# The byte positions of a weight ring in SBUF, moved stage by stage

## The reference

```python
# first block
z = rmsnorm(x) @ w_in                          # 1024 -> 4608
a = silu(layernorm(conv31(a_val * sigmoid(a_gt)))); y_a = a @ w_a_out
s = sc_b * conv3(sc_c * sc_v);                      y_b = s @ w_b_out
x = x + (sigmoid(.) * y_a + sigmoid(.) * y_b) @ w_o
u = rmsnorm(x) @ w_up                          # 1024 -> 2 * 2816
x = x + (gelu(conv3(u[:2816])) * u[2816:]) @ w_down
x = x + sigmoid(rmsnorm(x) @ w_ple_gate) * (p @ w_ple)
x = rmsnorm(x)
# second block
proj = rmsnorm(x) @ w_in_2                     # 1024 -> 2304, two kinds of attention
x = x + rmsnorm(attention(proj) @ w_out_2)
u = conv3(rmsnorm(x) @ w_up_2)                 # 1024 -> 2 * 4096
x = x + rmsnorm((gelu(u[:4096]) * u[4096:]) @ w_down_2)
```

## The kernel before

| operand | before | after |
|---|---|---|
| weights of in, b_out, ple, a_out, o | 96 | 80 |
| weights of up, down | 96 | 48 |
| weights of gate, in2, out2 | 96 | 72 |
| weights of up2 and the first three units of down2 | 96 | 56 |
| weights of the other 29 units of down2 | 0 | 0 |
| chunks h, h2 (also the operand of o) and f | 0 | 0 |
| chunks s, a, p and y | 64 | 0 |

## Time and profile before

### The profile page before, as it was taken

The page is one execution under the profiler, slowest core; times in us unless marked ns, Lnnn a source line. Parts: engine busy times, 40 slices in busy tenths (PEclk is TensorE's granted clock), DMA queues, the critical chain, the costliest instruction groups (busy, mean ns, idle before and its releaser), DMA issues. The chain is left out here.

```text
span 790.7 us, 17002 instructions
## 1 busy us (share of the span) xinstructions
PE 763.4 (97%) x5986; PEld 735.0 (93%) x5986; DVE 584.8 (74%) x1051; ACT 449.0 (57%) x752; POOL 259.6 (33%) x159
## 2 busy tenths in 40 slices
PE   8999999999999999999899998799999999999996
PEld 8999999999999999999788887699999999988885
DVE  6899967668888885436866785679999999963333
ACT  7554555566565664446744565576666666653441
POOL 0376642462122213345480011822211222122220
PEclk9999999999999999999999999899999999999999
DMA  8566554556555576644343332535555555666551
GB/s 278 160 213 197 189 161 146 190 184 191 192 181 194 184 236 210 193 138 143 131 133 109 106 108 77 165 107 186 189 187 185 189 187 187 218 201 196 188 171 53
DMA packets 37772, 135.46 MB, mean 171 GB/s; under 512 B 4448, under 2 KB 4704, under 8 KB 37728
## 3 DMA queue, kind: packets, MB, share of 16 engines
q1 hardware_dynamic: 37728, 134.86, 52.3%
HBM read 133.80 MB, written 1.05 MB: 171 GB/s over the span
## 5 line engine op out<-in xcount | busy, mean ns | idle before, releaser
L1655 PE MATMUL bank<-h_hi,w_hi 128*128 128x256 f32 x1424 | 403.7, 283 | 9.2 <-DVE h_lo L1072 6.5
L1656 PE MATMUL bank<-h_lo,w_hi 128*128 128x256 f32 x1424 | 399.1, 280 | 0.0
L1657 PE MATMUL bank<-h_hi,w_lo 128*128 128x256 f32 x1424 | 398.9, 280 | 0.0
L718 ACT ACTIVATE w_hi<-raw 128x1024 fp32r<-128x1024 f32 (+2 forms) x246 | 262.1, 1067 | 92.4 <-PE bank L1657 43.1
L553 POOL TENSOR_TENSOR w_lo<-raw,w_hi 128x1024 fp32r<-128x1024 f32 (+1 forms) x75 | 186.4, 2487 | 383.9 <-ACT w_hi L718 383.6
L1060 DVE TENSOR_TENSOR w_lo<-raw,w_hi 128x1024 fp32r<-128x1024 f32 (+2 forms) x171 | 218.3, 1279 | 104.4 <-ACT w_hi L718 104.3
L1655 PEld LDWEIGHTS bank<-h_hi,w_hi 128*128 128x128 f32 x1424 | 269.5, 189 | 16.2 <-issue 9.1
L1656 PEld LDWEIGHTS bank<-h_lo,w_hi 128*128 128x128 f32 x1424 | 269.7, 189 | 0.0
L1657 PEld LDWEIGHTS bank<-h_hi,w_lo 128*128 128x128 f32 x1424 | 269.4, 189 | 0.0
L1100 DVE TENSOR_TENSOR bank<-bank,scales 128x256 f32<-128x256 f32 x124 | 53.0, 431 | 27.8 <-PE bank L1657 13.9
L1328 DVE TENSOR_TENSOR f_lo<-src,f_hi 128x256 f32 (+1 forms) x54 | 60.7, 1124 | 0.5 <-ACT f_hi L866 0.5
(11 more groups left out here) (203 smaller groups left out, 914.4 us busy)
## 6 DMA issues: line engine op xcount, KB each, us to landing
raw<-in_w_up SPq DMA_DIRECT2D x108, 512.0 KB, 3.3
raw<-in_w_in SPq DMA_DIRECT2D x54, 512.0 KB, 3.4
raw<-in_w_down SPq DMA_DIRECT2D x32, 512.0 KB, 4.2
raw<-in_w_down SPq DMA_DIRECT2D x16, 704.0 KB, 4.1
raw<-in_w_o SPq DMA_DIRECT2D x8, 512.0 KB, 3.3
raw<-in_w_gate SPq DMA_DIRECT2D x8, 512.0 KB, 3.5
raw<-in_w_out SPq DMA_DIRECT2D x8, 512.0 KB, 3.3
raw<-in_w_b_out SPq DMA_DIRECT2D x4, 512.0 KB, 3.6
```

The source lines that it names most:

```text
L718: nc.scalar.activation(w_hi[s][:, cols], raw[s][:, cols], ACT.Copy).then_inc(hi_ready, 1)
L1655: nc.tensor.matmul(ps, wh, hi[:, k, :], start=start and n == 0, stop=False)
L1656: nc.tensor.matmul(ps, wh, lo[:, k, :], start=False, stop=False)
L1657: last = nc.tensor.matmul(ps, wl, hi[:, k, :], start=False, stop=stop and n == len(ks) - 1)
```

## The change

The ring gets another position, and that position another one for each stage. `w_hi` and `w_lo` become slices of one tensor `w_all` whose first slot starts 48 bytes past a multiple of 128 (`RING_COL = 12` floats); `first_col` adds 8, 0, 6, 2 or 20 floats by the stage, and now counts in every load, rounding, subtraction and product. `raw` lies behind `w_all` and uses the same columns. Large tensors start at multiples of 128 instead of 64 bytes, which moves s, a, p and y (table above). Four pairs of small scratch values share two tensors (`lam`, `o_small`). No instruction is added or removed, and the order, the semaphores and all shapes stay. The rest of the diff passes the unit instead of its slot to `products`, in every call.

```diff
@@ -55,12 +55,18 @@
 
 WARM_UP = 16
 
-RING_PAST = 32
+RING_COL = 12
 
 
 def first_col(u):
 
-    return RING_PAST // 4 if u >= UNIT0["down2"] + LEAD else 0
+    if u < UNIT0["up"]:
+        return 8
+    if u < UNIT0["gate"]:
+        return 0
+    if u < UNIT0["up2"]:
+        return 6
+    return 2 if u < UNIT0["down2"] + LEAD else 20
 
 
 def unit_blocks(u):
@@ -267,15 +273,15 @@
         at = [(nc.sbuf_base + 31) // 32 * 32]
 
         def aligned(offset, size):
-            step = 64 if size >= 1024 else 32
+            step = 128 if size >= 1024 else 32
             return (offset + step - 1) // step * step
 
-        def sb(name, shape, dt=f32, offset=None, past=0):
+        def sb(name, shape, dt=f32, offset=None, small=False):
 
             size = 4 * math.prod(shape[1:])
             if offset is not None:
                 return nc.alloc_sbuf_tensor_at(name, shape, dt, offset=offset)
-            at[0] = aligned(at[0] - past, size) + past
+            at[0] = aligned(at[0], 0 if small else size)
             t = nc.alloc_sbuf_tensor_at(name, shape, dt, offset=at[0])
             at[0] += size
             return t
@@ -285,8 +291,8 @@
         gg = sb("gg", [P, DC])
...
         UNIT_MAX = max(b for _, _, b in PHASES) * P
-        raw = [sb(f"raw{i}", [P, UNIT_MAX], past=RING_PAST) for i in range(RING)]
-        w_hi = [sb(f"w_hi{i}", [P, UNIT_MAX], f32r, past=RING_PAST) for i in range(RING)]
-        w_lo = [sb(f"w_lo{i}", [P, UNIT_MAX], f32r, past=RING_PAST) for i in range(RING)]
+        ring_at = (at[0] - 4 * RING_COL + 127) // 128 * 128 + 4 * RING_COL
+        w_at = ring_at - ring_at % 32
+        w_all = sb("w_all", [P, 2 * RING * UNIT_MAX + 8], f32r, offset=w_at)
+        w_first = [(ring_at - w_at) // 4 + UNIT_MAX * i for i in range(2 * RING)]
+        w_hi = [w_all[:, w_first[i]:w_first[i] + UNIT_MAX] for i in range(RING)]
+        w_lo = [w_all[:, w_first[RING + i]:w_first[RING + i] + UNIT_MAX] for i in range(RING)]
+        at[0] = w_at + 4 * (2 * RING * UNIT_MAX + 8)
+        raw = [sb(f"raw{i}", [P, UNIT_MAX], small=True) for i in range(RING)]
         X = sb("X", [P, DC, TOK])
         branch = sb("branch", [P, DC, TOK])
         h_hi = sb("h_hi", [P, DC, TOK], f32r)
-            load("in", 0, (0, None))
+            load("in", 0, (0, None), first_col(0))
...
-                    load(name, i, (slot(base + i), (base + i) // RING))
+                    load(name, i, (slot(base + i), (base + i) // RING), first_col(base + i))
...
-            def products(ps, s, block0, ks, hi, lo, start, stop, ready=None):
+            def products(ps, u, block0, ks, hi, lo, start, stop, ready=None):
 
                 for n, k in enumerate(ks):
                     if ready is not None:
                         pe.wait_ge(*ready(k))
-                    b = block0 + n
-                    wh, wl = (w[s][:, b * P:(b + 1) * P] for w in (w_hi, w_lo))
+                    col = first_col(u) + (block0 + n) * P
+                    wh, wl = (w[slot(u)][:, col:col + P] for w in (w_hi, w_lo))
...
-                    products(bank[slot(t)][:, 0:TOK], slot(u), 0, range(DC), hi, lo, True, True,
+                    products(bank[slot(t)][:, 0:TOK], u, 0, range(DC), hi, lo, True, True,
```

More of the change, by code:

```diff
@@ L287, in build @@
         ones_over = sb("ones_over", [P, P + 3])
-        lsum = sb("lsum", [P, 2])
-        lexp = sb("lexp", [P, 2])
+        lam = sb("lam", [P, 4])
+        lsum, lexp = lam[:, 0:2], lam[:, 2:4]
         neg_lam = sb("neg_lam", [P, 1])
@@ L500, in _ @@
                          ).then_inc(g_first_in, 16)
-            load("in", 0, (0, None))
+            load("in", 0, (0, None), first_col(0))
             for n in range(4):
                 load_x(n)
-            load("in", 1, (1, None))
-            load("in", 2, (2, None))
+            load("in", 1, (1, None), first_col(1))
+            load("in", 2, (2, None), first_col(2))
             sp.dma_start(ident[:], d["ident"]).then_inc(ident_in, 16)
-            load("in", 3, (3, None))
+            load("in", 3, (3, None), first_col(3))
             sp.dma_start(vec[:], d["vec"]).then_inc(vec_in, 16)
@@ L1291, in _ @@
             dve.wait_ge(lam_step, 1)
-            nc.vector.reduce_sum(lsum[:], lprod[:], axis=AX.X).then_inc(lam_step, 1)
+            nc.vector.reduce_sum(lsum, lprod[:], axis=AX.X).then_inc(lam_step, 1)
             for i in range(4):
@@ L1716, in first_pair @@
                             bank_free(t + n)
-                        last = products(bank[slot(t + n)][:, 0:TOK], slot(u + n), first,
+                        last = products(bank[slot(t + n)][:, 0:TOK], u + n, first,
                                         range(first, end), hi, lo, first == 0, end == DC,
@@ L1739, in _ @@
                     first = DC // 2
-                    products(bank[slot(u)][:, 0:TOK], slot(u), 0, range(first), hi, lo, True, False)
+                    products(bank[slot(u)][:, 0:TOK], u, 0, range(first), hi, lo, True, False)
                     pe.wait_ge(memset_done, 3)
                     mean_squares("in")
-                products(bank[slot(u)][:, 0:TOK], slot(u), first, range(first, DC), hi, lo,
+                products(bank[slot(u)][:, 0:TOK], u, first, range(first, DC), hi, lo,
                          first == 0, True, ready).then_inc(unit_done, 1)
@@ L1752, in _ @@
                     bank_free(24 + n, it, RING)
-                    products(bank[slot(24 + n)][:, 0:TOK], slot(24 + n), 0, range(DC), h_hi, h_lo,
+                    products(bank[slot(24 + n)][:, 0:TOK], 24 + n, 0, range(DC), h_hi, h_lo,
                              True, True).then_inc(unit_done, 1)
@@ L1758, in _ @@
                 bank_free(u)
-                products(bank[slot(u)][:, 0:TOK], slot(u), 0, range(DC), h_hi, h_lo, True, True
+                products(bank[slot(u)][:, 0:TOK], u, 0, range(DC), h_hi, h_lo, True, True
                          ).then_inc(unit_done, 1)
@@ L1775, in paired_units @@
                 for half in range(2):
-                    last = products(bank[slot(t)][:, half * TOK:(half + 1) * TOK], slot(u), half * k,
+                    last = products(bank[slot(t)][:, half * TOK:(half + 1) * TOK], u, half * k,
                                     range(k), hi, lo, True, True,
@@ L1800, in up_units @@
                     bank_free(t + RING, it - 1, per_it[n % 2])
-                    products(bank[slot(t)][:, 0:TOK], slot(u), 0, range(DC), h_hi, h_lo, True, True
+                    products(bank[slot(t)][:, 0:TOK], u, 0, range(DC), h_hi, h_lo, True, True
                              ).then_inc(unit_done, 1)
@@ L1826, in down_tile @@
                             bank_free(t, it, 2 if per_tile == 2 else 1)
-                    products(bank[slot(t)][:, 0:TOK], slot(u), 0, range(k * r, k * r + k),
+                    products(bank[slot(t)][:, 0:TOK], u, 0, range(k * r, k * r + k),
                              f_hi, f_lo, r == 0, r == per_tile - 1, ready).then_inc(unit_done, 1)
@@ L1841, in project @@
                     first = DC // 2
-                    products(bank[slot(t)][:, 0:TOK], slot(UNIT0["in2"] + u), 0, range(first),
+                    products(bank[slot(t)][:, 0:TOK], UNIT0["in2"] + u, 0, range(first),
                              h2_hi, h2_lo, True, False)
                     broadcast_rsqrt("final")
-                products(bank[slot(t)][:, 0:TOK], slot(UNIT0["in2"] + u), first, range(first, DC),
+                products(bank[slot(t)][:, 0:TOK], UNIT0["in2"] + u, first, range(first, DC),
                          h2_hi, h2_lo, first == 0, True).then_inc(unit_done, 1)
@@ L1920, in out2_part @@
                     bank_free(t)
-                last = products(bank[slot(t)][:, 0:TOK], slot(u), first, range(first, end),
+                last = products(bank[slot(t)][:, 0:TOK], u, first, range(first, end),
                                 y_hi, y_lo, first == 0, end == DC, chunk_ready("y"))
@@ L1964, in _ @@
                 for n in range(2):
-                    last = products(bank[slot(t + n)][:, 0:TOK], slot(u + n), k, [k], h_hi, h_lo,
+                    last = products(bank[slot(t + n)][:, 0:TOK], u + n, k, [k], h_hi, h_lo,
                                     k == 0, k == DC - 1, deferred_ready("up2") if n == 0 else None)
@@ L1973, in _ @@
                     broadcast_rsqrt("up2")
-                products(bank[slot(t + n)][:, 0:TOK], slot(u + n), 0, range(DC // 2), h_hi, h_lo,
+                products(bank[slot(t + n)][:, 0:TOK], u + n, 0, range(DC // 2), h_hi, h_lo,
                          True, False)
@@ L1977, in _ @@
                     mean_squares("up2")
-                products(bank[slot(t + n)][:, 0:TOK], slot(u + n), DC // 2, range(DC // 2, DC),
+                products(bank[slot(t + n)][:, 0:TOK], u + n, DC // 2, range(DC // 2, DC),
                          h_hi, h_lo, False, True).then_inc(unit_done, 1)
```

5 lines of the change are left out of this document (3 added, 2 removed).

## The result

The changed kernel is a little slower: 796.59 us (795.73 to 799.12, 8 runs) against 793.81 (792.71 to 796.26, 8 runs), a ratio of 1.0036 with a 95% interval of [1.0021, 1.0051]. The forecast was 8 us faster. Of the rivals it is C, slower in up, down and up2, that has the direction and the place; its size was too large.

The account below looks back on a forecast made before the run. TensorE, busy 763.4 of 790.7 us, was taken as the bound. Gains of 6.4 us (h, f), 1.1 (s, a, p) and 0.6 (y) sum to 8.1, taking the median from 794.5 to 786.4 us; range 769 to 805.

Parts of the forecast that it names:

- rival C: Products of h and f, above all in up, down and up2: weight load caught more often, 800.4 to 810.5 us; chance 0.23.
- The pace hangs on the difference of the positions: TensorE's matmuls: moving operand's start minus stationary one's, modulo 128 bytes, read as a cause of pace, 116.7 against 120.0 ns.
- rival B: No effect on h and f; only s, a, p and y come down to 116.7 ns, 1.1 us, 793.4 us; chance 0.16.
- Down2: Its 384 matmuls with moving weights keep their position difference: 0 us gained, pace to stay at 226.8 ns.
- The preparations and loads: Rounding, subtractions and loads at positions that are no multiple of 32 bytes: extra cost taken as 0.
- VectorE did not become the bound: Rival D, up2: subtractions a quarter longer, 0.32 us, make VectorE set the time, 797.6 us; chance 0.06.
- the new four lie around half the 128, as far from both as can be: New differences 48, 56, 72, 80 avoid bad places 0 and 96: h and f gain 1.33 ns per matmul, 6.4 us.
- a picture of two streams that catch up with each other: Moving stream and weight load: same bytes at 0, catching up at 96, least overhead at 32, where the moving stream starts ahead.
- the straight line: Pace rising evenly between differences 32 and 96 would make things worse, above all in up; the forecast argued against it.
- The terms of s, a, p and y: Their matmuls fall to 115.33 ns: s, a, p from 120.0, 1.1 us; y from 118.3, 0.6 us.
- The first units of down2: First three units go from difference 96 to 56: up to 6.7 ns per matmul, 0.2 us, left out of the sum.
- The lines of 16 bytes: By the skill's penalty for crossing lines, up2, gate, in2 and out2 touch 33 lines instead of 32 and would be worse.

## Why the prediction was wrong

**Held.** TensorE sets the time. The pace hangs on the difference of the positions (shown by the kernels with the weights back at d = 32 and with everything 64 bytes further), though not on it alone. At d = 80 up ran at 118.10 ns in three traces of three, at 32 at 116.67 in six of six; up2 ran at 117.78 in four of four at 72, and at 116.67 in four of five at 32. That speaks against rival B. The Trainium skill (SBUF — State Buffer, "Who interferes with whom") says that TensorE's two read ports are independent and that it never waits on anyone. The traces do not bear that out for these matmuls: over all runs one shape took 113.3 to 123.3 ns. Down2 kept its 87.1 us. The preparations and loads cost nothing more, though the prediction's reason was in part wrong: in the stages from in to down the loads still went to multiples of 32 bytes. VectorE did not become the bound (584.8 us busy, as before).

**The step that failed** is "the new four lie around half the 128, as far from both as can be", from which 1.33 ns per matmul were to be gained. Measured against 116.67: 0 at 48, 0.1 at 56, +1.1 at 72, +1.4 at 80. Up, down and up2 lost 1584 x 1.43 + 1536 x 1.11 ns = 4.0 us, where 3120 x 1.33 = 4.1 us of the 6.4 were to be gained: the largest term of the sum had the wrong sign. The mean over h and f is 116.67 + 4.0 / 4800 = 117.5 ns, above the 117.3 that rival C named as its point. C also named the place, up, down and up2; it took too much (118 to 120 ns, 5.9 to 16 us) because it read the pace of d = 96 as that of 72 and 80.

**Why it failed.** Three points (0, 32, 96) were joined by a picture of two streams that catch up with each other. Two of them were not what they seemed: 0 was read from down2's matmuls of 512 columns, and 96 stood for y as well, which lay at 224. The map between them is not smooth: 116.7, 120.0 and 116.7 at 32, 40 and 48. The three points could not tell the picture from the straight line, nor either from what is there. The size had no row either: of the two units in the earlier trace rows neither was faster than the usual pace (117.8 and 116.7 ns from their starts), so their difference was a loss that could end, and was booked as a gain below 116.7.

**The terms of s, a, p and y** were 1.1 and 0.6 us; by the paces they came to 240 x 1.3 = 0.3 and 192 x 1.6 = 0.3, and out2 as a whole still took 0.2 us more. They were counted modulo 128. Modulo 256 s, a and p went to 176, not to 48, and at 176 the pace is 118.65; where a kernel did give them 48 they ran at 116.7.

**The first units of down2** were to gain at d = 56 instead of 96. Modulo 256 they went from 224 to 184, and nothing moved: 233.2 ns before, 233.1 after, from their starts (32 intervals each).

**The lines of 16 bytes.** The Trainium skill (SBUF — State Buffer, "Door 1: The DMA port swizzle") gives 16-byte lines, by which the stages starting 8 past a line should be the worse ones. The trace does not agree: up2 (8 past one) ran at 117.8, up (on one) at 118.1, and gate and y (8 past one) at 116.8.

**What stays open** is the mechanism: why 40 is slow and 32 and 48 are not, what chooses among the rhythms of one d, what gives the order of three passes, and whether down2's moving weights could run below 226.7 ns. All other places tried for its units after the first three were slower (232.4 at 128, 233.0 to 233.3 at 8, 32, 64 and 192).

## What to carry to other kernels

When TensorE is the bound and its matmuls run back to back, divide a long stretch by its starts and compare equal shapes: a difference of a nanosecond can come from where the two operands lie against each other. Over the 5232 matmuls here it is worth 5.2 us, 0.7% of the kernel. Don't extrapolate such a pace from a few positions; scan them, each stage at another position in one run, and count positions modulo 256 bytes or more. Look at several traces before choosing, since one position can have two rhythms or more.

## What the runs showed of the hardware

Not expected: at one distance, 64, matmuls of 256 columns in fp32r run at 113.3 or at 117.8 ns for hundreds of matmuls, and with a restart every 96 matmuls the quick rhythm came exactly every third time. At d = 32, up2 ran at 116.67 in the kernel before and in three of the others, and at 117.78 in one. The single starts tell more than the mean. At 113.3 ns they lie 113 or 114 ns apart all the way; at 116.67 they go 120, 114, 116, 117 ns over and over in up2 of the kernel before; in the long stretch at 123.3 they alternate between about 117 and 130. Five paces, 113.33, 116.67 and 120.0 and, for 512 columns, 226.67 and 233.33 ns, are 272, 280, 288, 544 and 560 cycles of 2.4 GHz, all multiples of 8, and the granted clock was 1.00 in each of the stretches. The other paces of the table, 117.78 or 118.10 for two, are none, so this is a remark and not a rule.
